# One layer kernel: value rows of the expert retrieval multiplied by a diagonal of coefficients on TensorE, with a value ring of eight rows

## What is computed

```python
def peer(x, w_q, keys, w_u, w_v):
    q = (xt @ w_q).reshape(T, PEER_HEADS, 2, PEER_HALF)
    s_half = jnp.einsum('thcd,hcnd->thcn', q, keys)
    ...                       # top 16 of 128 twice, top 16 of their 256 sums, softmax: expert, gate
    def run(blk):
        xc, ec, gc = blk
        u = jnp.take(w_u, ec, axis=0)
        h = jnp.einsum('cd,ced->ce', xc, u)
        a = jax.nn.gelu(h, approximate=False) * gc
        return jnp.einsum('ce,ced->cd', a, jnp.take(w_v, ec, axis=0))
    ...
h = layer_norm(DN_ALPHA * h + peer(h, ...), ln2_g, ln2_b)
```

## Time and profile before

| | |
|---|---|
| median of 3 runs | 3723.6 us (3716.94 to 3732.24) |
| profiled execution, span | 3707.8 us |
| TensorE busy | 2594.1 us, 70% |
| VectorE busy | 2232.9 us, 60% |
| ScalarE busy | 1620.7 us, 44% |
| GpSimd busy | 2138.6 us, 58% |
| mean granted TensorE clock | 0.839 |
| DMA | 1219.35 MB, 329 GB/s over the span |

### The profile page before, as it was taken

One profiled execution on the slowest core, in us unless ns is written; L12 is line 12 of the kernel. 1 busy time (PEld: TensorE's weight loads), 2 busy tenths in 40 slices (PEclk: granted clock), 3 DMA queues, 4 the chain that ended last, 5 costly groups with the idle time before them and its releaser, 6 DMA issues.

```text
span 3707.8 us, 41225 instructions
## 1 busy us (share of the span) xinstructions
PE 2594.1 (70%) x14180; PEld 2145.3 (58%) x14180; DVE 2232.9 (60%) x5046; ACT 1620.7 (44%) x1839; POOL 2138.6 (58%) x2063
## 2 busy tenths in 40 slices
PE   7999965777996665778886656768876744544445
PEld 4468654566765654657756645657756643434444
DVE  5252266877656666776666666766566574565543
ACT  1121133555544444555554444555454443434434
POOL 1000055776766556786875556777665566666664
PEclk9999986887998887888988877889988876666667
DMA  5013398999999999999999999999999999999997
GB/s 210 24 72 120 122 350 328 355 348 356 409 409 375 357 350 339 365 347 370 409 409 370 351 350 349 349 336 394 409 402 361 343 345 354 339 344 349 342 351 293
DMA packets 341765, 1219.35 MB, mean 329 GB/s; under 512 B 37874, under 2 KB 47091, under 8 KB 341172
## 3 DMA queue, kind: packets, MB, share of 16 engines
q0 software_dynamic: 294912, 1073.87, 77.1%
q1 hardware_dynamic: 34980, 118.92, 8.7%
q10 hardware_dynamic: 11664, 23.92, 1.7%
HBM read 1204.25 MB, written 12.32 MB: 328 GB/s over the span
## 4 chain that ended last, share of the span: by engine, by line
PE 41%; another core or an unknown queue 22%; ACT 15%; issue 10%; POOL 5%; DMA 3%; DVE 3%; DVEq 1%; ACTq 0%
PE acc L735 19%; ACT av L1315 11%; PE mB L660 3%; PE fA L603 3%; POOL rows L371 3%; PE fA L561 2%; POOL rows L362 2%; PE mB L579 2%; PE fB L615 2%; PE fB L400 1%; DMA rows<-in_peer_v,ids_peer 1%; DMA rows<-in_peer_u,ids_peer 1%; PE fA L626 1%; ACT L1306 1%
## 5 line engine op out<-in xcount | busy, mean ns | idle before, releaser
L735 PE MATMUL acc<-ident,av 128*128 128x128 f32 x8192 | 1301.7, 318 | 1001.3 <-ACT av L1315 626.2
L735 PEld LDWEIGHTS acc<-ident,av 128*128 128x128 f32 x8192 | 1136.3, 166 | 1180.4 <-ACT av L1315 701.5
L1315 ACT ACTIVATE av<-rows,coef 128x1024 f32<-128x1024 f32 x1024 | 1157.2, 1146 | 1367.0 <-remote 745.0
L371 POOL DMA_INDIRECT rows<-in_peer_v,ids_peer x1024 | 1069.5, 1044 | 766.2 <-ACT av L1315 497.8
L362 POOL DMA_INDIRECT rows<-in_peer_u,ids_peer x1024 | 1050.8, 1026 | 650.0 <-DVE ids_peer L1034 312.7
L1054 DVE CUSTOM_DVE_ANT_0 rows<-rows,fB 128x1024 f32<-128x1024 f32 x538 | 650.0, 1217 | 450.7 <-DMA rows<-in_peer_u,ids_peer 410.5
L1054 DVE CUSTOM_DVE_ANT_0 rows<-rows,hh 128x1024 f32<-128x1024 f32 x486 | 586.4, 1221 | 225.0 <-DMA rows<-in_peer_u,ids_peer 162.7
L603 PE MATMUL fA<-hT_g,wring 128*128 128x256 f32 x1024 | 242.4, 390 | 6.2 <-issue 6.1
L660 PE MATMUL mB<-hT_g,wring 128*128 128x256 f32 x1024 | 242.9, 392 | 1.1 <-ACT hT_g L1277 1.1
L603 PEld LDWEIGHTS fA<-hT_g,wring 128*128 128x128 f32 x1024 | 196.6, 197 | 36.1 <-issue 10.3
L660 PEld LDWEIGHTS mB<-hT_g,wring 128*128 128x128 f32 x1024 | 200.0, 201 | 27.5 <-ACT hT_g L1277 1.3
(11 more groups left out here) (203 smaller groups left out, 2269.0 us busy)
## 6 DMA issues: line engine op xcount, KB each, us to landing
wring<-in_wstream SPq DMA_DIRECT2D x192, 512.0 KB
rows<-in_peer_u,ids_peer POOLq DMA_INDIRECT x1024
rows<-in_peer_v,ids_peer POOLq DMA_INDIRECT x1024
hT_spill<-rows ACTq DMA_DIRECT2D x1, 4096.0 KB
wring<-in_wstream SPq DMA_DIRECT2D x16, 256.0 KB
hT_g<-hT_spill ACTq DMA_DIRECT2D x4, 1024.0 KB
out_h<-ybuf ACTq DMA_DIRECT2D x8, 512.0 KB
S<-in_w_lat SPq DMA_DIRECT2D x1, 2048.0 KB, 11.6
```

Source lines behind the costliest of these rows:

```text
L371: pool.indirect_dma_start(v_rows[:, ring(g, i, NV), :], None, peer_v, bass.IndirectOffsetOnAxis(ap=ids_peer[:, t, s:s + 1], axis=0)).then_ ...
L735: last = mm(acc[:, tok(k)], av[:, i % NAV, tok(k)], ident[:, :], is_transpose=True, start=i % SLOTS == 0 and k % 4 == 0, stop=i % SLOTS == ...
L1315: s.activation(av[:, i % NAV, :], v_rows[:, ring(g, i, NV), :], ACT.Copy, scale=coef[:, b, i % BATCH:i % BATCH + 1]).then_inc(scaled, 1)
```

## The change

ScalarE no longer scales the v row. It multiplies the 128x128 identity by the slot's coefficients (one for each partition) into one of `ND` = 8 tiles `diag`, and TensorE multiplies the landed v row by this diagonal in two products of 128x512, straight into `acc`, which now holds positions on partitions and needs no turning back. The tiles `av` and `ybuf` go; the v ring gets eight rows, and start-up tiles that lay in `av` and `ybuf` now lie in its last two rows. TensorE frees the v row (`v_free`), VectorE finishes a tile from `acc` into `h1_peer`, and the store reads `h1_peer`, one semaphore for each tile. `finish` runs two steps sooner, and the front no longer waits for `y_read`.

```diff
--- before.py
+++ after.py
@@ -41,8 +41,8 @@
 LEAD = 40
 PAIRS = PH // 2
 PSLOTS = SLOTS // PAIRS
-NU = NV = 6
-NAV = 2
+NU, NV = 6, 8
+ND = BATCH
 NW = 4
 EVEN, HALFK = S // 4 + 1, S // 4
 WQ0, WM0, WO0, WP0 = 0, 4, 4 + 3 * KD, 4 + 4 * KD
@@ -119,7 +119,7 @@
         hh = sb("hh", [P, 2 * TILES, D])
         h1_front, h1_peer = hh[:, 0:TILES, :], hh[:, TILES:2 * TILES, :]
         hT_g = sb("hT_g", [P, KD, GROUP])
-        av = sb("av", [P, NAV, D])
+        diag = sb("diag", [P, ND, P])
         ln = sb("ln", [P, 4, D])
         keysT = sb("keysT", [P, 2 * PH, NK])
         yo = sb("yo", [P, 2, D])
@@ -127,7 +127,6 @@
         oT = yo[:, 1, :].rearrange("p (c t) -> p c t", c=4)
         cqT_g = sb("cqT_g", [P, 2, GROUP])
         o_sb = sb("o_sb", [P, H * VD])
-        ybuf = sb("ybuf", [P, D])
         ident = sb("ident", [P, P])
         qcT = sb("qcT", [P, 2, GROUP])
         rope_g = sb("rope_g", [P, GROUP])
@@ -183,8 +182,9 @@
         w_z_sb = wring[:, :, :].rearrange("p a b -> p (a b)").rearrange("p (k n) -> p k n", k=KD)
         dft_sb = ln[:, 2:4, :]
         mid_sgn, mid_row = yo[0:1, 0, 0:EVEN], yo[0:1, 0, 512:1024]
-        w_kr_sb = av[:, 0, 0:512].rearrange("p (k n) -> p k n", k=KD)
-        dftc = av[:, 1, 0:2 * FD]
+        w_kr_sb = rows[:, NU + NV - 2, 0:512].rearrange("p (k n) -> p k n", k=KD)
+        dftc = rows[:, NU + NV - 2, 512:512 + 2 * FD]
+        ybuf = rows[:, NU + NV - 1, :]
         w_uk_sb = ln[:, 0, :].rearrange("p (k n) -> p k n", k=2)
         w_uv_sb = ln[:, 1, :].rearrange("p (k n) -> p k n", k=2)
         ln0 = KT[:, 0:3, :]
@@ -213,7 +213,6 @@
         fA, fB = ps("fA", 1024), ps("fB", 1024)
         mB = ps("mB", 1024)
         m0, m1 = mB[:, 0:512], mB[:, 512:1024]
-        turned_to = (mB, fA)
         lat_banks = (m0, acc[:, 0:512])
         banks = (fA[:, 0:512], fA[:, 512:1024], fB[:, 0:512], fB[:, 512:1024])
 
@@ -259,10 +258,11 @@
         first_handed, handed, h1_handed = sem("first_handed"), sem("handed"), sem("h1_handed")
         u_in = [sem(f"u_landed{i}") for i in range(NU)]
         v_in = [sem(f"v_landed{i}") for i in range(NV)]
-        u_free, scaled, y_read = sem("u_free"), sem("scaled"), sem("y_read")
+        u_free, v_free, y_read = sem("u_free"), sem("v_free"), sem("y_read")
         act_done, coef_done = sem("act_done"), sem("coef_done")
-        av_free, yT_sb, y_ps = (sem(n) for n in ("av_free", "yT_sb", "y_ps"))
-        var2, std2, out_ready, stored = (sem(n) for n in ("var2", "std2", "out_ready", "stored"))
+        diag_done = sem("diag_done")
+        var2, std2, out_ready = (sem(n) for n in ("var2", "std2", "out_ready"))
+        stored = [sem(f"stored{t}") for t in range(TILES)]
 
         block = ctx.enter_context(nc.Block())
 
@@ -366,7 +366,9 @@
             def gather_v(g, i):
                 g, i = slot_of(g, i)
 
-                pool.wait_ge(scaled, g * STEPS + i + 1)
+                pool.wait_ge(v_free, g * STEPS + i + 1)
+                if g == 0 and i == NV - 1:
+                    pool.wait_ge(cq_spilled, 16 * (GROUPS - 1))
                 t, s = divmod(i, SLOTS)
                 pool.indirect_dma_start(
                     v_rows[:, ring(g, i, NV), :], None, peer_v,
@@ -400,8 +402,8 @@
                 return nc.tensor.transpose(out_, in_, ident[:, :])
 
 
-            for _ in range(NAV):
-                pe.nop().then_inc(av_free, 1)
+            for _ in range(NV):
+                pe.nop().then_inc(v_free, 1)
             pe.wait_ge(ident_read, 16)
 
             def turn_h0(i):
@@ -555,8 +557,6 @@
                         if u == 0:
                             if positive(g * TILES):
                                 pe.wait_ge(h1T_sb, g * TILES)
-                            if g > 1:
-                                pe.wait_ge(y_read, (g - 1) * TILES)
                         for half in range(2):
                             last = mm(fA[:, half * 512:(half + 1) * 512], qT_g[0:QK, h, tok(qt)],
                                       KT[0:QK, h, half * 512:(half + 1) * 512], start=True, stop=True)
@@ -651,8 +651,6 @@
                         if qc == 0:
                             pe.wait_ge(h1T_sb, (g + 1) * TILES)
                             pe.wait_ge(oT_sb, (g + 1) * TILES)
-                            if g > 0:
-                                pe.wait_ge(y_read, (g - 1) * TILES + 1)
                         if positive(g * 2 * PH + qc - 1):
                             pe.wait_ge(qc_sb, g * 2 * PH + qc - 1)
                         w = chunk(g, WP0 + qc)
@@ -729,22 +727,14 @@
             def peer(g, i):
                 g, i = slot_of(g, i)
                 if i % SLOTS == 0 and positive(g * TILES + i // SLOTS):
-                    pe.wait_ge(yT_sb, g * TILES + i // SLOTS)
-                pe.wait_ge(scaled, NV + g * STEPS + i + 1)
-                for k in range(KD):
-                    last = mm(acc[:, tok(k)], av[:, i % NAV, tok(k)], ident[:, :], is_transpose=True,
-                              start=i % SLOTS == 0 and k % 4 == 0, stop=i % SLOTS == SLOTS - 1, skip_group_check=True)
-                last.then_inc(av_free, 1)
-
-            def turn_back(g, t):
-                pe.wait_ge(yT_sb, g * TILES + t + 1)
-                pe.wait_ge((oT_sb, h1T_sb)[t], min(g + 2, GROUPS) * TILES)
-                if positive(g * TILES + t):
-                    pe.wait_ge(y_read, g * TILES + t)
-                for k in range(KD):
-                    last = mm(turned_to[t][:, tok(k)], ybuf[:, tok(k)], ident[:, :], is_transpose=True,
-                              start=k % 4 == 0, stop=True, skip_group_check=True)
-                last.then_inc(y_ps, 1)
+                    pe.wait_ge(y_read, g * TILES + i // SLOTS)
+                pe.wait_ge(diag_done, g * STEPS + i + 1)
+                pe.wait_ge(v_in[ring(g, i, NV)], landed(g, i, NV))
+                for half in range(2):
+                    cols = slice(half * 512, (half + 1) * 512)
+                    last = mm(acc[:, cols], diag[:, i % ND, :], v_rows[:, ring(g, i, NV), cols],
+                              start=i % SLOTS == 0, stop=i % SLOTS == SLOTS - 1)
+                last.then_inc(v_free, 1)
 
             for m in range(STEPS):
                 front(0, m)
@@ -756,9 +746,6 @@
                 dft(m)
             for g in range(GROUPS):
                 for m in range(STEPS):
-                    for t in range(TILES):
-                        if m + LEAD == (t + 1) * SLOTS + 1:
-                            turn_back(g, t)
                     if g + 1 < GROUPS:
                         front(g + 1, m)
                     if has_slot(g, m + LEAD, g + 1 == GROUPS):
@@ -984,6 +971,8 @@
                     if alone:
                         number_experts(t, 0, 1, m, FIRST_ALONE, first_handed)
                     if m == (FIRST_ALONE if alone else id_steps[q])[3] and q == 0:
+                        if g > 0:
+                            dve.wait_ge(stored[t], 16 * g)
                         v.tensor_copy(h1_peer[:, t, :], h1_front[:, t, :]).then_inc(h1_handed, 1)
                     if m == id_steps[q][0]:
                         dve.drain()
@@ -1060,20 +1049,21 @@
                 k = i // BATCH
                 dve.wait_ge(act_done, g * (STEPS // BATCH) + k + 1)
                 if positive(g * STEPS + BATCH * (k - 1)):
-                    dve.wait_ge(scaled, NV + g * STEPS + BATCH * (k - 1))
+                    dve.wait_ge(diag_done, g * STEPS + BATCH * (k - 1))
                 t, s0 = divmod(k * BATCH, SLOTS)
                 v.tensor_tensor(coef[:, k % 2, :], act_out[:, k % 2, :], gate_peer[:, t, s0:s0 + BATCH],
                                 ALU.mult).then_inc(coef_done, 1)
 
             def finish(g, t):
-                dve.wait_ge(y_ps, g * TILES + t + 1)
-                v.scalar_tensor_tensor(out=ybuf[:, :], in0=h1_peer[:, t, :], scalar=ALPHA, in1=turned_to[t][:, :],
+                dve.wait_ge(v_free, NV + g * STEPS + (t + 1) * SLOTS)
+                v.scalar_tensor_tensor(out=h1_peer[:, t, :], in0=h1_peer[:, t, :], scalar=ALPHA, in1=acc[:, :],
                                        op0=ALU.mult, op1=ALU.add).then_inc(y_read, 1)
                 dve.drain()
-                stats(2, ybuf, var2)
+                stats(2, h1_peer[:, t, :], var2)
 
             def finish_norm(g, t):
-                normalise(2, ybuf[:, :], ybuf[:, :], std2, g * TILES + t + 1, ln[:, 2, :], ln[:, 3, :], out_ready)
+                normalise(2, h1_peer[:, t, :], h1_peer[:, t, :], std2, g * TILES + t + 1, ln[:, 2, :], ln[:, 3, :],
+                          out_ready)
                 dve.drain()
 
             def peer(g, m, last):
@@ -1140,9 +1130,9 @@
                 for m in range(STEPS):
                     peer(g, m, last)
                     for t in range(TILES):
+                        if m + LEAD == (t + 1) * SLOTS:
+                            finish(g, t)
                         if m + LEAD == (t + 1) * SLOTS + 2:
```

(32 more changed lines are left out.)

## The result

On the chip of the first measurement the changed kernel takes 3621.0 us (median of four runs, 3610.7 to 3628.0) where the kernel before takes 3725.9: ratio 0.973, 95% interval 0.970 to 0.976. Forecast were 3630 us. On another chip the changed kernel takes 3462.5 us and the kernel before 3406.6: ratio 1.017 (1.014 to 1.020), slower. Both have to be explained.

What follows compares the result with a forecast made beforehand. Row gathers near the DMA limit, starved in light stretches by ScalarE's wait on late completions. Rounds -35, last round -56 and -6, first steps -5, finish +10, end -2: -94, span 3614, median 3630 us; range 3465 to 3800.

Steps and rivals of the forecast that it cites:

- A, E, F, G: Steps 0-84 (attention), 161-224 (retrieval queries), 225-255 per round, last round's 0-148: -16, -19, -13 each round, -56 us.
- H: The 67 steps at the end, mostly without u gathers: 2.5 to 2.4 us a step, -6 us.
- first slots: The first 40 steps, before round 0, counted as light: -5 us.
- B, C and D: Steps 85-132 (gates, branch outputs), 133-148 (output projection), 149-160 (LayerNorm): +25, +11.5 us and unchanged, each round.
- TensorE's slot (4): Two products replace eight transposes: 1.72 us a slot at full clock, making TensorE the bound of attention, gates and output projection.
- the 94% of TensorE: Share of time TensorE was taken to be busy in attention and gates, giving 2.90 and 3.69 us a step.
- late completions go on ruling: Rival: light stretches stay as they are, heavier products are paid in full, 3859 us; decided past 13 us lateness; chance 0.17.
- step (2): ScalarE's wait: an eight-slot loop replaces the two-slot one, covering late completions up to 13 us, so light stretches reach the next limit.
- step (3): Next limit of feeding in light stretches, by DMA rate or packet share: F 2.70, G 2.69, E 3.00 us a step.
- ScalarE (1): 1024 scalings of 1.15 us become diagonal writes of 0.36: 1157 to about 370 us, by itself no gain.
- half clock: Rival: TensorE stays at 1.2 GHz in the light end stretches, 3.43 us a slot, about 3975 us; chance 0.05.
- Finish (5): At tile ends VectorE reads `acc` itself and the next tile's first product waits: +10 us (0 to +30).

Runs made afterwards that it cites:

- e2_nv6: Changed kernel with a value ring of six rows instead of eight: 3599.3 us, ratio 0.977.
- e1_nd2: Changed kernel with two diagonals instead of eight, the ring of eight rows kept: 3620.4 us, ratio 0.983.
- e3_av3: Kernel before with a third tile of scaled rows and a value ring of five rows instead of six: 3659.1 us, ratio 0.995.
- e4_half: Changed kernel without the second product of 128x512, except in a tile's first and last slot: 3522.1 us, ratio 0.957.
- r_before: Kernel before, unchanged, run again for its trace on another chip: 3721.3 us.
- e7_short: Changed kernel with the last round's gathers fetching rows for 64 of 128 positions, on the second chip: 3456.7 us, ratio 1.015.

## Why the prediction was right, and where it wasn't

The span was forecast at 3614 us and is 3620.1. That it comes so near is luck: two errors of nearly the same size cancel. By the table the light stretches (A, E, F, G, H, first slots) were to give 211 us and gave 127, and B, C and D were to take 110 and took 41.

**TensorE's slot (4)**: 1.72 us forecast, 1.80 in B at clock 1.00, 1.92 in C at 0.97. The rest of TensorE's work in B was smaller, (165.69 - 86.46)/48 = 1.65 in place of 1.75. The step that failed is the 94% of TensorE: it was 99% in B. Presumably the v rows that wait in the ring keep it fed. So a step took 3.48 us and not 3.69; C took 3.75 and not 4.03 in round 1.

**D left as it is** was wrong: 35 to 27 us in round 1, 116 to 79 in three. Before, D was bound by feeding (409 GB/s). After, C runs behind the feeding (333 GB/s), the ring is full of landed rows when D begins, and TensorE works them off: 12 slots with 20 gathers, ten pairs. What a heavy stretch holds up is partly given back in the next one. C and D together went from 256 to 261 us, where 291 were forecast. The ring's part in it shows in e2_nv6: with six rows D takes 91 us in place of 79. This term was sized by a stage alone, and a boundary between stages is no wall.

**Light stretches (2, 3)**: forecast A -48, E -57, F -39, G -56, measured -16, -35, -34, -33. The bound of 13 us up to which the ring of eight covers a late completion was about right (14 of the 16 pauses in G end 12.9 us or more after the product's end). The size of the lateness was not: I had it from one stall, 8.6 us, and here it reaches 13 us once in some ten slots (14 pauses in 149). The 8.6 us were misread, too: they are ScalarE's idle time, and from the transposes' modelled end to the scaling it is 3252.98 - 3245.43 = 7.55 us. The rival *late completions go on ruling* thus came true in part, by the very condition that was written for it; the four light terms were each too large, by 32, 22, 5 and 23 us. And the loop of two tiles, on which step (2) rests, was not alone what held the kernel: with two diagonals the light stretches keep their gain (e1_nd2), and a third tile brings 23 us (e3_av3). On the second chip, where nothing is late, the terms of step (3) and (4) come out as forecast or lower: A 738 (a forecast of 2.90 us a step is 740), E 555, F 2.53 us a step, G 2.61, at 406 GB/s. They were right as limits. The kernel before takes 3407 us there, 319 less than where it was first measured, so presumably it meets the same limits and the edit has nothing left to win; what stands alone then is the products' cost in B and C less D's part, 33 + 43 - 37 = 39 us by the table, of the 56 us that the changed kernel loses. The trace of the kernel before is missing there, so this is argued and not shown, and 17 us have no place.

**ScalarE (1)**: 390 ns and 344 us, forecast 0.36 and 370. **Clock**: G stands at 0.95 and the second chip's at 0.99, so *half clock* is out. (The argument that full stretches are granted 1.00 was too broad: the earlier trace rows has a full one of 5 us at 0.56.) It wasn't the step from transposes to products by itself that raised it: the eight transposes a slot of before had 0.68 in G, one product a slot has 0.62 (e4_half), two have 0.95. **Finish (5)**: VectorE's read of `acc` waits for the product line in these eight cases (idle before it in the last columns),

```profile
L1059 DVE SCALAR_TENSOR_TENSOR hh<-hh,acc 128x1024 f32<-128x1024 f32 x8 | 9.8, 1220 | 57.6 <-PE acc L735 51.3 <-issue 6.1 <-remote 0.2
```

and TensorE's product waits for that read

```profile
PE acc L735 <- DVE hh L1059: 5.2, 3, 2.6
```

5.2 us in all: the low part of 0 to +30, below the +10 taken. What VectorE's own 51.3 us of waiting cost the u side isn't shown. **H** was to gain 6 and lost 2.

## What to carry to other kernels

Trading another engine's work for TensorE's has a price wherever TensorE is full, and what it buys can hang on the chip: here the edit gains 2.7% on a chip where TensorE's completions arrive late, and on one where they don't it loses 1.7%. Before such a trade, size a wait from the whole distribution in the trace and not from one stall, and compare the records' ends with the starts of the engines that wait and with the semaphore's updates; count the updates first, since some may be missing. Cost a heavy stretch together with the light one behind it, because a ring gives part of the delay back.

## What the runs showed of the hardware

- The same kernel takes 3407 us on one chip and 3682 to 3726 on others. No completion of TensorE's peer line is over 1 us late on the one (0 of 1024, changed kernel); on the others 39% (e1_nd2) to 54% (r_before) are by the recorded updates, and 20 and 42% by the bound of the waiting engines. The Trainium skill ("TensorE: Matmul & The Clock Gate", "The cost: per-tile semaphore tail") gives the tail of a semaphore increment in tens of ns. The second chip doesn't exceed that (0.01 us after the modelled end); on the others the measured lateness, up to some 16 us, is of another order.
- In the last round lateness didn't change with the DMA engines' load (share 0.97 or 0.65) nor with TensorE's (72 or 84% busy), but it goes with the number of gathers started just before.
- The granted clock in G is 0.68 with eight transposes of 128x128 a slot, 0.62 with one product of 128x512 and 0.95 with two. One product takes 1.75 us a slot there (260.9/149), two take 2.04.
- Rows for 64 partitions move at half the rate: G of e7_short on the second chip has DMA full with half of the bytes.

```profile
q0 software_dynamic: 12593, 41.26, 100.1%
```

That is the queue of gathers in 3050 to 3250 us (packets, MB, share of 16 engines): 41.26 MB in 200 us are 206 GB/s at 100%, where the unchanged kernel moves 80.04 MB at 101%. The Trainium skill ("SBUF — State Buffer", "Door 1: The DMA port swizzle") says that the rate depends on how many of SBUF's ports the partitions reach, and by its table the first 64 reach half of them; the trace agrees. Half rows to all partitions do relieve the engines (185 GB/s at 0.65).
